# Gating of u begins four units earlier, and the last gelu of u follows the casts of V's first two rows

## The reference, cut to what matters

```python
sc = einsum('thpc,hpnc->thpn', q, subkeys)        # 8 heads x 2 halves x 128 keys
top_s, top_i = top_k(sc, 16)
cand = top_s[:, :, 0, :, None] + top_s[:, :, 1, None, :]
best_s, best_pos = top_k(cand, 16)                # 16 of 256 pairs of keys
idx, gate = ..., softmax(best_s)
a = gelu(einsum('td,ted->te', x, u[idx]))         # u: 16384 x 1024
y = einsum('te,ted->td', a * gate, v[idx])        # v: 16384 x 1024
```

## Time and profile before

| | |
|---|---|
| median of 3 runs | 2416.84 us (2416.06 to 2418.9) |
| the profiled execution, its time | 2417.25 us |
| its span in the trace | 2415.4 us |
| PE busy | 2309.0 us, 96% |
| DVE busy | 1439.9 us, 60% |
| ACT busy | 1136.3 us, 47% |
| POOL busy | 911.4 us, 38% |
| granted clock of PE, mean | 0.974 |

### The profile page before, as it was taken

How to read it: one execution, slowest core, us unless ns; L and a number is a source line. 1 busy time by engine, 2 the same in 40 slices (tenths; PEclk the granted TensorE clock), 3 DMA queues, 4 the chain that set the end, 5 groups by cost and what they waited for, 6 DMA issues and landing times.

```text
span 2415.4 us, 50540 instructions
## 1 busy us (share of the span) xinstructions
PE 2309.0 (96%) x17336; PEld 2140.5 (89%) x17336; DVE 1439.9 (60%) x2714; ACT 1136.3 (47%) x2231; POOL 911.4 (38%) x754
## 2 busy tenths in 40 slices
PE   7889999999999999999999888999999999999997
PEld 6754554789999999999999877899999999999997
DVE  6404444326916999655555644269169996555555
ACT  5523332155664444455555542556644444555554
POOL 5621111077987666100000150679876661000000
PEclk9999999999999999999999998999999999999999
DMA  4487777544554444455555631445544444555552
GB/s 161 135 236 303 291 299 296 203 158 148 182 182 149 139 137 136 144 182 177 180 182 182 189 140 61 158 149 183 180 149 137 137 138 146 177 179 182 181 178 102
DMA packets 105488, 420.79 MB, mean 174 GB/s; under 512 B 12101, under 2 KB 12701, under 8 KB 95945
## 3 DMA queue, kind: packets, MB, share of 16 engines
q1 hardware_dynamic: 92728, 335.28, 41.2%
q0 software_dynamic: 12400, 83.47, 9.9%
q10 hardware_dynamic: 288, 1.08, 0.1%
HBM read 375.14 MB, written 44.63 MB: 174 GB/s over the span
## 4 chain that ended last, share of the span: by engine, by line
PE 90%; issue 3%; DVE 2%; POOL 2%; ACT 1%; DMA 1%; POOLq 0%; ACTq 0%; DVEq 0%; SPq 0%
PE pa L392 62%; PE pb L392 28%; POOL split L1669 2%; DMA raw<-in_units 1%; DVE big L1498 0%; ACT big L900 0%; DVE top L1202 0%; DVE big L1600 0%; DVE big L1596 0%; DVE big L1610 0%; ACT split L872 0%; PE pb L783 0%; PE pb L631 0%; DVE big L1194 0%; DVE halves L1498 0%
## 5 line engine op out<-in xcount | busy, mean ns | idle before, releaser
L872 ACT CAST split<-raw 128x512 fp32r<-128x512 f32 x1176 | 721.0, 620 | 926.4 <-PE pa L392 647.4
L392 PE MATMUL pa<-xh,split 128*128 128x264 f32 x5280 | 993.0, 287 | 43.0 <-DVE xl L1214 24.0
L1669 POOL TENSOR_TENSOR split<-raw,split 128x512 fp32r<-128x512 f32 x664 | 862.5, 1306 | 311.0 <-ACT split L872 286.0
L392 PEld LDWEIGHTS pa<-xh,split 128*128 128x128 f32 x5280 | 832.3, 190 | 48.3 <-issue 25.4
L392 PE MATMUL pa<-xl,split 128*128 128x264 f32 x2640 | 753.5, 285 | 0.0
L1221 DVE TENSOR_TENSOR split<-raw,split 128x512 fp32r<-128x512 f32 x512 | 354.2, 692 | 304.6 <-ACT split L872 304.6
L392 PEld LDWEIGHTS pa<-xl,split 128*128 128x128 f32 x2640 | 503.7, 191 | 0.0
L392 PE MATMUL pa<-wsplit,split 128*128 128x264 f32 x3072 | 417.7, 285 | 6.6 <-DVE wsplit L1416 6.6
L392 PE MATMUL pb<-wsplit,split 128*128 128x264 f32 x3072 | 416.1, 284 | 0.0
L392 PEld LDWEIGHTS pa<-wsplit,split 128*128 128x128 f32 x3072 | 393.2, 189 | 6.9 <-issue 6.9
L392 PEld LDWEIGHTS pb<-wsplit,split 128*128 128x128 f32 x3072 | 391.9, 189 | 0.0
(11 more groups left out here) (262 smaller groups left out, 1633.6 us busy)
## 6 DMA issues: line engine op xcount, KB each, us to landing
raw<-in_units SPq DMA_DIRECT2D x636, 512.0 KB, 3.3
big<-in_state_in POOLq DMA_DIRECT2D x20, 1024.0 KB, 8.0
out_state_out<-big POOLq DMA_DIRECT2D x20, 1024.0 KB, 5.3
halves<-in_state_in POOLq DMA_DIRECT2D x12, 1024.0 KB, 8.7
out_state_out<-halves POOLq DMA_DIRECT2D x12, 1024.0 KB, 5.4
out_c_prompt<-big POOLq DMA_DIRECT2D x4, 1024.0 KB, 5.1
bias_rows<-scb POOLq DMA_DIRECT2D x1, 3072.0 KB, 39.0
big<-in_skeys POOLq DMA_DIRECT2D x2, 1024.0 KB, 7.6
```

Of the source, the lines that this page charges most:

```text
L392: return pe.matmul(out, lhs, rhs, start=start, stop=stop)
L872: nc.scalar.copy(split[:, 2 * (n % 2) + half, 0, :], ring[:, slot, half * 512:(half + 1) * 512]).then_inc(high_done, 1)
L1669: nc.gpsimd.tensor_tensor(split[:, v, 1, :], ring[:, (a + k) % RING, o], split_f[:, v, 0, :], ALU.subtract).then_inc(low_done["pool"], 1)
```

## The change

`EXP_AT`, `TURN_AT` and `SPREAD_AT` are each four units lower, so `SPREAD_TO` is 124: gate set 32 comes behind unit 123. On PE units 124 to 127 then follow it. On ACT the gelu of unit 127 moves behind `w_high` of rows 0 and 1, and the wait for the last gated row moves behind the first four units of V. On DVE there are 68 rows to take instead of 64, of which 124 to 126 come behind the last apply, and row 127 behind `w_low` of row 1. Fewer rows of ones are written by ACT (52, not 56 for each layer), and the memset covers 16 rows, not 8.

```diff
-EXP_AT = 56
-TURN_AT = 60
-SPREAD_AT = 64
+EXP_AT = 52
+TURN_AT = 56
+SPREAD_AT = 60
 SPREAD_TO = SPREAD_AT + 4 * (SETS // 2)
...
-            with act.Fori(1, (NK - SPREAD_AT) // RING) as it:
+            with act.Fori(1, (NK - SPREAD_AT) // RING - 1) as it:
                 for k in range(RING):
                     u_row(it, SPREAD_AT + k)
+            for i in range(NK - RING, NK - 1):
+                u_row(0, i)
             group[0] += NK
-
-            act.wait_ge(sem("row_gated"), n_r + NK - SPREAD_AT)
-            act.wait_ge(sem("gates_applied"), SETS * (L + 1))
             n0 = n_split(U_V[L])
...
+            act.wait_ge(sem("gates_applied"), SETS * (L + 1))
             w_high(None, 0)
             w_high(None, 1)
+            u_row(0, NK - 1)
             for k in range(RING):
                 high_at(U_V[L] + k + 2)
                 w_high(None if k < 2 else 0, k + 2)
+            act.wait_ge(sem("row_gated"), n_r + NK - SPREAD_AT)
             with act.Fori(1, NK // RING - 1) as it:
...
             low(U_V[L] % RING, nv, 2 * nv + 1)
             dve.wait_ge(sem("row_gated"), n_r + SPREAD_TO - SPREAD_AT)
             apply(0, SETS - 1)
-            for i in range(SPREAD_TO, NK):
-                take_row(0, i, n0 + SETS)
-
...
+            for i in range(SPREAD_TO, NK - 1):
+                take_row(0, i, n0 + SETS)
             w_low(0, 0)
             low((U_V[L] + 1) % RING, nv + 1, 2 * (nv + 1) + 1)
             w_low(0, 1)
+            take_row(0, NK - 1, n0 + SETS)
```

## The result

| | before | after |
|---|---|---|
| median | 2418.09 us (2416.06 to 2419.18, 6 runs) | 2407.6 us (2406.38 to 2410.01, 6 runs) |
| profiled execution, its time | 2417.25 us | 2407.88 us |
| its span | 2415.4 us | 2406.1 us |

The ratio of after to before is 0.9959, with a 95% interval of 0.9946 to 0.9972: 10 us, or 0.4%, faster. The forecast was 2411.2 us with a range from 2408.8 to 2415.4; the sign was right, the size was not.

A forecast was written before the change was run, and what follows sets the result against it. PE, busy 96% of the span, was taken as the bound. V's earlier start (1.16 us a layer) plus clock gains, with one fall, gave 5.6 us: 2411.2 us against the 2416.84 us median, range 2408.8 to 2415.4 us.

The forecast's parts named there:

- PE's path at the end of u: Between u and V: PE's gap shrinks from 3.29 to 1.97 us, ended by the gelu; V starts 1.16 us earlier a layer.
- The cover of the three rows: DVE before V: rows 124 to 126 and `w_low` end 0.5 us before the gelu, so they cost nothing.
- rival B: DVE before V: rows 124 to 126 at 1.20 us each delay PE, 1.0 us lost a layer, 2418.8 us; chance 0.06.
- The clock in V: V's first unit: a half-clock fall costs 1.6 us instead of 2.44; gain 0.84 us a layer with a fall, 2.44 without.
- One fall of two: Start of V: the clock falls in one layer only, 5.6 us gained in all; the likeliest case, chance 0.38.
- The three rows on DVE: DVE between the last apply and `w_low` of row 0: rows 124 to 126 take 0.43 us each and cost nothing.
- the choice four units earlier: Exponentials and transposes move together: 35 us of DVE's first wait remain, the second is unchanged; cost nothing.
- the memset: DVE's memset doubles, 1.82 us more, covered by its wait for the exponentials; cost nothing.
- straight code: Four more units of straight code on PE: zero cost, at worst a few tenths of a us.
- a term put at nothing: Beyond V's start and the clock behind the gap, the sum gave no gain, including in the stage between the layers.
- Rival C: End of u: something unseen holds the last apply or V's start; gain 0 to 3 us, 2415.3 us; chance 0.12.

The follow-up runs named there:

- gelu first: The change with ACT's old order, the gelu of unit 127 ahead of `w_high` of rows 0 and 1: 2408.38 us, ratio 0.9962.
- low later: The change with the `low` of V's unit 1 behind `w_low` of row 1 on DVE instead of ahead of it: 2407.99 us, ratio 0.9962.
- the change with either idle time: The change plus a DVE memset between V of layer 0 and the norm: 700 columns (0.93 us), 2411.51 us; 2750 columns (about 2.4 us), 2412.11 us.
- the last apply first: The change with the last apply and rows 124 and 125 ahead of the `low` of V's unit 0 on DVE: 2408.38 us, ratio 0.9961.
- 0.19 us of idle: 64-column DVE memset after layer 0's V, added to the kernel with the last apply first and V's first unit writing pb first: 2403.48 us, ratio 0.9946.
- the change with 2750 columns: The change plus a DVE memset of 2750 columns (about 2.4 us) between V of layer 0 and the norm: 2412.11 us, ratio 0.9984.

## Why the prediction was wrong

- **PE's path at the end of u: right.** The gap was forecast at 1.97 us, ended by the gelu, and is 1.79 us. The start of V comes 1.49 us earlier a layer instead of 1.16. Of the 0.33 us between them 0.15 is PE's end of u, for which I had added the longer last matmul, and the rest lies in `w_high`, the cast behind it and the release of PE, each some hundredths shorter than summed. In two layers it is 0.65 us of 10. The cover of the three rows was put a little too high: `w_low` releases PE in 0.27 us and the gelu in 0.14, so rival B would have bound from 0.37 us on, not 0.5.
- **The clock in V: right.** One fall of two was taken, 3.28 us; 3.60 us were measured. The 1.6 us for a fall is the difference of 375.04 and 373.50 us, 1.54; the fall of before, put at 2.44 us, cost 2.5 and 2.6 us in the two stages of V, which is the 0.3 us. That it was always so much does not hold: with idle time added, layer 1 had the same gap of 3.29 us and a fall of 1.56 us (375.06 against 373.50). And it was not a coin: in all five profiles with gaps of 1.8 to 2.0 us (the change, gelu first, low later, and the change with either idle time) the fall came in layer 0 and not in layer 1. That just one of two was the case forecast is in part luck, for the prediction gave either layer the same chance, and nothing in it told them apart.
- **The three rows on DVE, the choice four units earlier, the memset, straight code: right.** The rows took 1.12 us for three. DVE's wait for the exponentials shrank from 48.8 to 34.3 us, its wait for PE's transposes stayed 5.6 us, and PE has no new wait.
- **The step that failed is a term put at nothing.** The sum has two terms a layer, the start of V and the clock behind the gap. Everything else behind the gap stands at zero, and no reason is given for the stage between the layers; the median's difference was taken for the sum of two places. The stage between V of layer 0 and u of layer 1 gave 3.5 us more, 35% of the gain, by reaching its half-filled stretches at another moment of PE's clock. The two runs with 0.93 us of idle show that this moment alone makes the stage 3 us longer or shorter. The rows for it were there: the attention's gaps of 1.83 us and more with a granted clock of 0.59 behind them were used, but only to price a fall at the changed place. Without that stage the gain between the profiles would be 6.6 us, one of the forecast's cases to within 1 us. The median would then be about 2411.1 us; that this is so near to 2411.2 is luck, since the base had moved as well, from 2416.84 us for three runs to 2418.09 for six.
- **Rival B** (the rows on the path) has nothing for it: the three rows lasted 0.43 us each, as on the row at 987.35. By the Trainium skill's rule on the shared port (SBUF — State Buffer, "Who interferes with whom") they had to be short, since POOL is idle there, and the trace agrees. **Rival C** pulled the range up to 2415.4 us when the miss was on the other side; no rival allowed for a gain outside the changed places.
- **The chances.** Faster had 0.55 because the likeliest case lay 0.8 us from the bound; the order of the cases was sound, their common offset was not.

What was not tried: the new order of ACT alone on the old constants, since there the gelu of unit 127 would wait for the last apply, which itself waits for that row. And that the first part is long once the half-speed stretch ends 8.45 us and not 8.3 us in is read off twelve profiles (8.0 to 8.3 us with about 16.0 us, 8.45 to 11.0 us with about 18.6, six of each). In the six long ones the clock falls again while the 40 products run (before: at 1448.8, the products from 1445.95 to 1451.43), in the short ones only behind them (the change: at 1449.5, the products until 1448.04). Why it falls at the one moment and not at the other is not shown.

## What to carry to other kernels

In a stage where PE's gaps of 2 to 4 us let it change between its two clock speeds, as in this attention, a microsecond gained ahead of the stage can return as plus or minus 3 us behind it: compare stages, not only totals, and don't credit an edit with what an unchanged stage did. An edit that looks worthless in the total (the last apply first) can be a real gain that such a stage has taken back; a small shift may return it, as 0.19 us of idle did for 2.0 us of the stage. And at a change of phase, look at which banks the first unit writes: begun with those that the last reader does not hold, the wait for the reader disappears.

## What was not expected of the hardware

- Idle time made the kernel faster: 0.93 us of it, ahead of the attention, took 3.3 us off the median (ratio 0.9989, 0.9980 to 0.9998) and 2.95 us off the stage.
- The time from the first products with the keys to the end of V in layer 1 was the same in the two profiles of the kernel before: 1850.11 and 1850.27 us. The code ahead of it, the same in all twelve profiles, ends anywhere from 542.99 to 547.95 us. Of the 2.2 us between the spans of those two 2.0 us come from there.
- That does not cover every execution. Of the 78 of the kernel before on record four took 2407.4 to 2409.6 us, as little as the change, and the twelve of the change with 2750 columns fall into two groups, seven from 2409.8 to 2412.6 us and five from 2414.4 to 2414.7. None of the four and none of the five was profiled, so where they differ is open, and a stage read from one profile tells of that execution.
- Gaps of 1.79 us were followed by a fall in one layer and by none in the other of the same execution; gaps of 1.04 us by none in two of two.
